# Attention in 32 items of a head pair and a query tile, halves of the array in turn, four banks for index scores

## What is computed

```python
proj = x @ w_in          # q, k, v of all branches, index q and k, and the gates
# A: for each query the 128 keys with the best index score
rel   = relu(einsum('bqhd,bsd->bqhs', q_idx, k_idx))          # 8 index heads of 32
score = where(pos_k <= pos_q, einsum('bqhs,bqh->bqs', rel, w_idx) * idx_scale, -inf)
sel   = top_k(score, 128);  softmax over the selected keys, with a slope per head
# B: window of 128 keys, a sink in the softmax, two query heads for one key head
# C: all earlier keys (with 512 tokens each query sees every earlier block), slope, softmax
# D: stick breaking, no softmax
z = q @ k.T * scale
log_keep  = where(pos_k < pos_q, log_sigmoid(-z), 0)
a = where(strict, exp(log_sigmoid(z) + cumsum_from_the_right(log_keep) - log_keep), 0)
y_d = a @ v
merged = sum_n(sigmoid(g_n) * (y_n @ w_branch_n));  out = merged @ w_out
```

## Time and profile before

| what | us |
|---|---|
| median of three runs | 1786.89 |
| time of the profiled execution | 1791.51 |
| its span, first to last instruction | 1789.5 |
| TensorE busy in the span | 1733.0 |
| DVE busy | 1354.5 |
| ACT busy | 766.8 |
| GpSimd busy | 756.8 |
| mean granted TensorE clock | 0.981 |

### The profile page before, as it was taken

How to read it: one execution, slowest core, us unless ns; L and a number is a source line. 1 busy time by engine, 2 the same in 40 slices (tenths; PEclk the granted TensorE clock), 3 DMA queues, 4 the chain that set the end, 5 groups by cost and what they waited for, 6 DMA issues and landing times.

```text
span 1789.5 us, 23990 instructions
## 1 busy us (share of the span) xinstructions
PE 1733.0 (97%) x8789; PEld 1504.8 (84%) x8789; DVE 1354.5 (76%) x2574; ACT 766.8 (43%) x1337; POOL 756.8 (42%) x426
## 2 busy tenths in 40 slices
PE   7999999989999999999999999989899999999995
PEld 5667777768888999999999999989788888888884
DVE  2358994372236599789888988778889898889888
ACT  4334344442223443675477377533334333333331
POOL 5222223234446467514522632356455465344333
PEclk9889999999999999999999999999999999999997
DMA  5111112124242356787588668999999999999991
GB/s 194 48 48 54 53 59 65 65 63 150 82 130 71 104 172 211 231 300 274 177 287 288 218 227 303 333 406 400 407 407 392 388 397 373 386 393 393 380 334 71
DMA packets 126355, 417.60 MB, mean 233 GB/s; under 512 B 12960, under 2 KB 32416, under 8 KB 124704
## 3 DMA queue, kind: packets, MB, share of 16 engines
q1 hardware_dynamic: 70176, 232.81, 36.6%
q0 software_dynamic: 36864, 134.23, 20.1%
q10 hardware_dynamic: 19200, 49.03, 7.4%
HBM read 364.91 MB, written 50.86 MB: 232 GB/s over the span
## 4 chain that ended last, share of the span: by engine, by line
PE 88%; DMA 5%; DVE 5%; ACT 1%; issue 1%; ACTq 0%; SPq 0%; DVEq 0%
PE ps L1276 16%; PE ps L1277 16%; PE ps L1278 16%; PE ps L1469 9%; PE ps L1470 9%; PE ps L1472 9%; PE ps L1568 5%; DMA gelu_in<-gelu_d 2%; PE ps L1348 2%; DMA u_got<-u_rows,eid 2%; PE ps L1392 2%; DMA raw<-u_units 1%; PE ps L1361 1%; PE ps L1367 1%; PE ps L1327 1%; DVE u_got L1070 1%
## 5 line engine op out<-in xcount | busy, mean ns | idle before, releaser
L1276 PE MATMUL ps<-tok_hi,w_hi 128*128 128x384 f32 (+2 forms) x1552 | 555.6, 358 | 17.5 <-DVE tok_lo L812 9.3
L1277 PE MATMUL ps<-tok_lo,w_hi 128*128 128x384 f32 (+2 forms) x1552 | 546.8, 352 | 0.0
L1278 PE MATMUL ps<-tok_hi,w_lo 128*128 128x384 f32 (+2 forms) x1552 | 546.4, 352 | 0.0
L537 ACT ACTIVATE w_hi<-raw 128x1024 fp32r<-128x1024 f32 x334 | 353.1, 1058 | 355.9 <-PE ps L1472 184.0
L437 POOL TENSOR_TENSOR w_lo<-raw,w_hi 128x1024 fp32r<-128x1024 f32 x80 | 194.0, 2429 | 365.2 <-ACT w_hi L537 365.0
L1276 PEld LDWEIGHTS ps<-tok_hi,w_hi 128*128 128x128 f32 x1552 | 295.9, 191 | 38.7 <-issue 11.8
L1278 PEld LDWEIGHTS ps<-tok_hi,w_lo 128*128 128x128 f32 x1552 | 295.7, 191 | 19.8
L1277 PEld LDWEIGHTS ps<-tok_lo,w_hi 128*128 128x128 f32 x1552 | 296.1, 191 | 17.9
L1469 PE MATMUL ps<-w_hi,gh_hi 128*128 128x512 f32 x768 | 299.8, 390 | 5.5 <-DVE gh_lo L1200 5.3
L1064 DVE TENSOR_TENSOR w_lo<-raw,w_hi 128x1024 fp32r<-128x1024 f32 x196 | 239.0, 1219 | 87.3 <-ACT w_hi L537 87.0
L493 POOL DMA_INDIRECT u_got<-u_rows,eid x128 | 169.1, 1321 | 309.1 <-DVE h_own L1070 298.6
(11 more groups left out here) (194 smaller groups left out, 1939.6 us busy)
## 6 DMA issues: line engine op xcount, KB each, us to landing
raw<-u_units SPq DMA_DIRECT2D x128, 512.0 KB, 4.1
raw<-v_rows SPq DMA_DIRECT2D x128, 512.0 KB, 8.5
raw<-w_units SPq DMA_DIRECT2D x78, 512.0 KB, 3.4
gate_d<-stage ACTq DMA_DIRECT2D x12, 2048.0 KB, 7.8
gelu_d<-gelu_t ACTq DMA_DIRECT2D x120, 192.0 KB, 4.0
gelu_in<-gelu_d SPq DMA_DIRECT2D x30, 768.0 KB, 9.3
gate_in<-gate_d SPq DMA_DIRECT2D x28, 768.0 KB, 15.5
gate_in<-gate_d SPq DMA_DIRECT2D x2, 1536.0 KB, 23.0
```

Of the source, the lines that this page charges most:

```text
L537: act.activation(w_hi[:, n % RAW, :], raw[:, n % RAW, :], ACT.Copy).then_inc(hi_done, 1)
L1276: pe.matmul(out_, l_hi, r_hi, start=start, stop=False)
L1277: pe.matmul(out_, l_hi, r_lo, start=False, stop=False)
L1278: return pe.matmul(out_, l_lo, r_hi, start=False, stop=stop)
```

## The change

The 16 heads become 8 pairs with 4 query tiles each, 32 items s, one per unit. For item s TensorE does scores of s+1, weights of s, outputs of s-1, the unit. Scores, probabilities, logarithms and `colw` of an item hold both heads side by side ([128, 2, 512]), and `row`, `ls` and `colw` are double. Where two operations of one engine were needed for two tiles of a head, one now takes both heads, except where a scale or a sum is per head. Head pair matmuls alternate between row halves (scores, banks 2 and 3) and column halves (outputs). D's scores now go by query tile, so a tile i has i+1 matmuls a head of 128 columns in place of one, and its sums (i+1)(i+2)/2 a head. B's heads are reordered to (0, 2, 1, 3), so that the two of a pair read different halves of the keys; the host permutes w_branch to match. Index scores take banks 2 to 5, and each waits for the relu four before it. V is transposed into the unit's own bank (n mod 2), and unit n+2 then waits for ACT to have read it. DVE's bias is computed for both heads, for A in each item.

```diff
-        [("B", h) for h in range(NH)] + [("A", h) for h in range(NH)]
+        [("B", h) for h in (0, 2, 1, 3)] + [("A", h) for h in range(NH)]
-    row = [at(f"row{i}", R + 84 + 5 * i, [P, 1280]) for i in range(4)]
-    colw = at("colw", R + 104, [P, 1280])
+    row = [at(f"row{i}", R + 84 + 4 * i, [P, 2, S]) for i in range(2)]
+    ls = [at(f"ls{i}", R + 92 + 4 * i, [P, 2, S]) for i in range(2)]
+    bias = ls[0]
+    colw = [at(f"colw{i}", R + 100 + 4 * i, [P, 2, S]) for i in range(2)]
...
@@ ACT @@
+            def exponents(s):
...
+                    act.wait_ge(nbias_set, soft_item(s) + 1)
+                    for ab in range(2):
+                        act.activation(row[s % 2][:, ab, :n], row[s % 2][:, ab, :n], ACT.Exp, scale=SCALE,
+                                       bias=nbias[:, ab, i:i + 1], accum_out=rsum[:, ab, i:i + 1]).then_inc(exp_done, 1)
...
+            def weights(s):
...
+                    act.wait_ge(t_full, s + 1)
+                    if s >= 2:
+                        act.wait_ge(pv_done, 2 * (s - 1))
+                    act.activation(colw[s % 2][:, :, :n], ps[:, 4:6, :n], ACT.Copy).then_inc(t_read_act, 1)
...
@@ DVE @@
+            def scores(s):
...
+                    dve.wait_ge(item_scores, 2 * (s + 1))
+                    dve.tensor_scalar(tmp[:, :, :n], ps[:, 2:4, :n], SCALE, None, ALU.mult).then_inc(item_read, 1)
...
+                    dve.scalar_tensor_tensor(ls[s % 2][:, :, :n], tmp[:, :, :n], -1.0, tmp[:, :, :n],
+                                             ALU.mult, ALU.min).then_inc(abs_set, 1)
...
+            for s in range(-1, N_ITEM):
+                if s + 1 < N_ITEM:
+                    scores(s + 1)
+                if s >= 0:
+                    weights(s)
+                if s >= 5 and s % 4 == 1:
+                    store_y(s // 4 - 1)
+                if s >= 0:
+                    for _ in range(2 + s % 2):
+                        if r < 3 * TOPK // 8:
+                            choose_keys(r)
+                            r += 1
+                if s + 1 < N_ITEM:
+                    scores_end(s + 1)
...
@@ TensorE @@
             def att_unit(n):
...
+                if n - 2 in V_UNITS:
+                    pe.wait_ge(vt_read, V_ORDER.index(n - 2) + 1)
...
             def index_scores(first):
...
-                    score_free(s)
-                    pe.matmul(score_bank(s)[:, :(t + 1) * P], projT[rows, 6 + h // 4, t * P:(t + 1) * P],
+                    if s >= 4:
+                        pe.wait_ge(relu_done, s - 3)
+                    pe.matmul(index_bank(s)[:, :(t + 1) * P], projT[rows, 6 + h // 4, t * P:(t + 1) * P],
...
+            def scores(s):
...
+                if s == 0:
+                    pe.wait_ge(relu_done, 3 * IH)
+                else:
+                    pe.wait_ge(item_read, s)
+                k0, n = keys_of(kind, i)
+                for kt in range(i + 1 if kind == "D" else 1):
+                    for ab in range(2):
+                        rows = slice(HD * ab, HD * ab + HD)
+                        q, k = projT[rows, q_slot, :], projT[rows, k_slot, :]
+                        if kind == "D":
+                            ins = pe.matmul(ps[:, 2 + ab, kt * P:(kt + 1) * P], k[:, kt * P:(kt + 1) * P], q[:, tile_],
+                                            start=True, stop=True)
+                        else:
+                            ins = pe.matmul(ps[:, 2 + ab, :n], q[:, tile_], k[:, k0:k0 + n], start=True, stop=True)
...
+            def weights(s):
...
+                if s >= 1:
+                    wait_t_read(s - 1)
+                if kind == "D":
+                    pe.wait_ge(softplus_set, s - 8 + 1)
+                    for ab in range(2):
+                        for kt in range(i + 1):
+                            for k2 in range(kt, i + 1):
+                                last = pe.matmul(ps[:, 4 + ab, kt * P:(kt + 1) * P],
+                                                 (neg_after if k2 == kt else neg_ones)[:],
+                                                 row[s % 2][:, ab, k2 * P:(k2 + 1) * P], start=k2 == kt, stop=k2 == i)
+                else:
+                    pe.wait_ge(probs_set, 2 * (soft_item(s) + 1))
+                    for ab in range(2):
+                        for j in range(keys_of(kind, i)[1] // P):
+                            block_ = slice(j * P, (j + 1) * P)
+                            last = pe.transpose(ps[:, 4 + ab, block_], row[s % 2][:, ab, block_], ident[:])
+                last.then_inc(t_full, 1)
+
+            def outputs(s):
...
+                for j in range(n // P):
+                    for ab in range(2):
+                        c0 = 0 if kind == "A" else HD * ab
+                        ins = pe.matmul(ps[HD * ab:HD * ab + HD, 6 + p % 2, i * P:(i + 1) * P],
+                                        v_tok[:, chunk, k0 // P + j, c0:c0 + HD], colw[s % 2][:, ab, j * P:(j + 1) * P],
+                                        start=j == 0, stop=j == n // P - 1)
...
+            for s in range(-1, N_ITEM):
+                n = N_FIRST + s
+                if s + 1 < N_ITEM:
+                    scores(s + 1)
+                if s >= 0:
+                    weights(s)
+                    if s >= 1:
+                        outputs(s - 1)
+                    if n < N_ATT:
+                        att_unit(n)
+                    if n - 1 in V_UNITS and n - 1 >= N_FIRST:
+                        v_to_tokens(n - 1)
+                for b in {29: (2, 3), 31: (1,)}.get(s, ()):
+                    branch(0, b)
+            outputs(N_ITEM - 1)
```

More of the change, by code:

```diff
@@ L846, in choose_keys @@
                     link(dve.tensor_tensor(left_over, left_over, dist[:, S - n:S], ALU.add))
[L848 to L851 removed]
+            def scores(s):
+                kind, i, p = kind_of(s), s % 4, s // 4
+                n = keys_of(kind, i)[1]
                 if kind != "D":
[L853 to L868 removed]
@@ new lines, in scores @@
+                    width = {"A": n, "B": 2 * P, "C": S}[kind]
+                    if s >= 2:
+                        dve.wait_ge(t_full, s - 1)
+                    dve.wait_ge(item_scores, 2 * (s + 1))
+                    for ab in range(2):
+                        ins = dve.tensor_tensor_reduce(
+                            out=row[s % 2][:, ab, :n], in0=ps[:, 2 + ab, :n], in1=bias[:, ab, width - n:width], scale=1.0,
+                            scalar=-3.0e38, op0=ALU.add, op1=ALU.max, accum_out=mx[:, ab, i:i + 1])
@@ L896, in scores_end @@
-                    link(dve.reciprocal(rinv[:, u % 2, two], rsum[:, u % 2, two]))
-                    for t in (2 * half, 2 * half + 1):
-                        n, o = keys_of(kind, t)[1], row_at(kind, t)
-                        dve.tensor_scalar(row[u % 2][:, o:o + n], row[u % 2][:, o:o + n], rinv[:, u % 2, t:t + 1],
+                        dve.wait_ge(sink_exp, 2 * (s - 16 + 1))
+                        link(dve.tensor_tensor(rsum[:, :, i], rsum[:, :, i], esink[:, :, i], ALU.add))
+                    link(dve.reciprocal(rinv[:, :, i], rsum[:, :, i]))
@@ L918, in weights @@
-            def weights(u, half):
-                if HEADS[u][0] != "D":
-                    return
-                for i in (2 * half, 2 * half + 1):
-                    kt = keys_scored(u, i)
-                    o, n = col_at(kt), S - kt * P
-                    idx = plan["u", u, i][0]
-                    dve.wait_ge(tp_full, idx + 1)
-                    dve.tensor_tensor(colw[:, o:o + n], ps[:, 4 + idx % 2, :n], row[2 + u % 2][:, o:o + n],
-                                      ALU.add).then_inc(tp_read_dve, 1)
+                    last = slice(i * P, (i + 1) * P)
@@ new lines, in scores_end @@
+                    softplus, logs = row[s % 2], ls[s % 2]
+                    dve.wait_ge(t_full, s - 1)
+                    dve.wait_ge(stick_ln, s - 8 + 1)
+                    link(dve.scalar_tensor_tensor(softplus[:, :, :n], tmp[:, :, :n], 0.0, logs[:, :, :n],
+                                                  ALU.max, ALU.add))
+                    dve.tensor_tensor(softplus[:, :, last], softplus[:, :, last],
+                                      seen[:].unsqueeze(1).to_broadcast([P, 2, P]), ALU.mult).then_inc(softplus_set, 1)
@@ L1630 @@
         [qb[:, :P], qb[:, P:], w["kb"], w["vb"]] + two("qa") + [cat(w["ka"], w["ka"])]
+    by_pair = a["w_branch"][0].copy()
+    by_pair[1] = by_pair[1].reshape(2, 2, HD, DM).transpose(1, 0, 2, 3).reshape(2 * P, DM)
     proj, units = iter(proj), []
```

370 lines of the change are left out of this document (116 added, 254 removed).

## The result

| | before | after |
|---|---|---|
| median of the runs, one comparison | 1786.57 us (1785.91 to 1789.42, 4 runs) | 1764.38 us (1761.96 to 1765.24, 4 runs) |
| profiled execution | 1791.51 | 1765.24 |
| its span | 1789.5 | 1763.2 |
| mean granted TensorE clock | 0.981 | 0.984 |

The ratio is 0.9863, with a 95% interval from 0.9846 to 0.9881: the kernel became faster by 1.4%, 24.5 us (21.3 to 27.5); the two medians differ by 22.2. The forecast was 1755, a gain of 31.8; the range of 1746 to 1774 holds the result. The two profiled executions differ by 26.3 us.

The account below looks back on a forecast made before the run. TensorE, busy 97% of the span, was taken as the bound. Gains of 18 (index scores and opening) and 17 (steps with a unit), less 4 (tail), gave 31 to 32 us off the 1786.9 median: 1755 us, range 1746 to 1774.

Parts of the forecast that it names:

- (a): Index scores, 33.9 to 85.2 us: four banks shorten six sets from 16.5 to 5.0 us, plus 3.5 from the clock.
- (b): Opening, 85.2 to 97.4 us: 12.1 us becomes about 9.3, gain 2.8, bounds 0 and 5.
- The slow units: Units at low clock after four index sets cost 7.0 us; bounds 0 and 7, half (3.5) taken as gain.
- (c): Steps with a unit, 97.4 to 354 us: paired scores and outputs overlap on array halves, net gain 17 us.
- I charge 4 us for both pairs, bounds 0 and 8: D's steps: TensorE waits for DVE's softplus in steps with tiles 1 and 2, costing 4 us.
- The stalls beside GpSimd: D's steps: one DVE pass stands still while GpSimd splits a weight, some 1.6 us a step, 6.4 per pair.
- (d): Tail, 354 to 371.7 us: item 31's chain lies open without units, cost 4 us, bounds 1 and 8.
- From 372 on nothing is touched, and it shifts: Everything after the attention, from 372 us on, keeps its length and only moves earlier.
- Rival 1: Outputs: column halves run one after the other, costing 15.8 us more; gain 20, 1767 us; chance 0.23.
- Rival 2: Neither 64-row halves nor column halves overlap; another 9 us lost, gain 11, 1776 us; chance 0.06.
- Rival 3: Each short matmul has a fixed cost of 12 ns, adding 2.1 us in the attention: 1757 us; chance 0.05.
- Rival 4: Clock falls in the items' steps, units cost 7.25 us in place of 5.5: 51 us, 1806 us; chance 0.06.

Follow-up runs that it names:

- the second and third execution of before: The kernel before, unchanged, profiled two more times in one execution each: 1789.87 and 1788.6 us.
- the moved choosing: Kernel after with DVE's 48 rounds of choosing placed elsewhere, none in the last nine items: 1760.99 us, ratio 0.9841 to the kernel before.

## Why the prediction was right and where not

**Bound, (a) and (b), predicted 18, measured 21.1.** The sets take 0.86, 0.64, 0.86, 0.86, 1.07 and 1.07 us, 5.4 in all where 5.0 was forecast (11.2 won); only the first takes 0.2 more than its columns and a start. The opening, from the last set's end to unit 9, takes 7.8 where 9.3 was forecast and 11.8 stood before: the wait for the relus is 2.07 as foreseen, and the softmax chain of two heads with 128 columns is shorter. Unit 9 stays slow (0.74), as forecast. The slow units were to give back half of 7.0 us. In this pair of executions they give back all that they cost, 6.4. (The 7.0 set 7.25, read from starts, against 5.5, read from the chain of waits; by starts a unit at full clock takes 5.66 to 5.69.) Against the other two executions of before unit 9 comes 18 us earlier, exactly the sum.

**The base.** "... which lies 4.6 us above the median of 1786.9. I subtract from the median", with half of the slow units given back, holds for the kernel as it mostly runs: the second and third execution of before have two slow units of 4 to 8, and the half was right on average, though for no reason that the prediction had. The median itself was low: three later comparisons gave 1788.46, 1789.46 and 1787.85. Some 2 of the 9.4 us between 1755 and 1764.4 are this. The other 7.3 are gain that wasn't there (31.8 against 24.5). Those two executions of before and the two of after differ by 23 to 25 us, the first pair by 26.3; the terms below give both where they differ.

**(c), predicted 17, measured 12.9** in the first pair of executions (256.8 to 243.9, from the first matmul of unit 9 to the end of unit 37) and 12.2 in the others. Here most of the miss lies. The halves are right to a few hundredths: scores of 512 columns 1.06 us, outputs of tile 3 1.02, where 1.1 and 1.0 stood. Taken away they cost 11.8 and 13.5 us, where 15.8 less DVE's waits was reckoned. In the chain of waits a unit behind the outputs takes 5.66 to 5.69 us, where one behind transposes took 5.49 (116.57 to 122.06 before); that is the 0.2 for the return to the full width, charged rightly. Four items of C take 31.2 us, the two heads took 34.4: the 3.2 of the sum. The step that failed is "I charge 4 us for both pairs, bounds 0 and 8": TensorE waited 5.6 there, and D's eight steps took 82.7 against 79.6 by the sum (four heads of 20.5, less twice 3.2, plus 4). The mechanism was the one foreseen, DVE late in the steps before the longer sums; the moved choosing removes it and wins 3.4 us. The stalls beside GpSimd, 1.6 a step or 12.8 by the sum, were 7 us in four of the eight steps; two of them fell on the mask that TensorE waits for. In the whole stage TensorE is idle for 6.1 us. Without that it would have won 19.1 where 21 were reckoned: the share of the first and last items that falls outside the stage, put at 2, was too small. Of three short waits for probabilities (1.4 us together, 5.6 less the tail's 4.2) only one, 0.5, lies in this stage; the others are in the opening and in the tail.

**(d), predicted 4, measured 4.8** (22.6 less 17.9). The forecast length was 21.9. The wait of 4.2 is near the working, but the clock wasn't in it: after the pause most of the pieces run at the lower clock, item 31's transposes 1.87 us instead of 1.02, item 30's outputs 1.48 instead of 0.81, and the stretch has 0.85 on average.

**"From 372 on nothing is touched, and it shifts"** is the other step that failed: 29.3 won at the merge, 26.3 at the end, and in the other executions 25.4 won at the start of the out product and 23.9 at the end. From there to TensorE's last instruction four executions with the old attention take 1267.9 to 1269.1 us, nine with the changed one 1269.0 to 1272.6 (the one with the scores on the same rows 1268.0). About 2 us are mostly lost there. The stretch from 1221 has a clock of 0.93 in the kernel after; at the same work the kernel before has 0.97, with the DMA queues as full:

```profile
1250.00:1300.00 50.00, 44.68 (x188) 35.85 (x188) 42.14 (x67) 16.33 (x21) 23.07 (x18) 0.97 1.03 407
```

But the clock isn't what is lost. Counted by the same matmul, the kernel after is ahead by 28.1 us at 1179.3, by 23.8 at 1246.9, and by 29.1 again at 1263.6. It is down to 26.5 at 1337.4, and from 1263.5 on both kernels have a clock of 1.00; only 1.1 us of it is a wait of TensorE, for DVE's `gh_lo`. What there depends on a start that is 25 us earlier stays open.

**The rivals.** Rival 1 (column halves in turn) is refuted by 1.02 against 1.89 us. The Trainium skill's page "TensorEngine Tiling (Array Packing)", Key Properties, was right about columns as about rows. Rival 2 falls with it. Rival 3: the 40 instructions of a tile's sums in D take 4.63 to 4.72 us and start 0.112 us apart, those of outputs on one half 0.109 to 0.110, where 128 columns need 0.107. So each has a cost of its own of 2 to 5 ns, not 12. The 60 cycles that the Trainium skill's page "TensorEngine Tiling (Array Packing)", Instruction Overhead, gives don't show in any row. Rival 4 (the clock falls in the items): 0.99 from 75.9 to 319.8, and 1.00 in D, with four changes of width a step.

The sign, the range and the order of the parts came out right. The likeliest value was 9.4 us too low: some 2 us by the base, 4 to 5 in the steps with a unit (3 of them D's), 1 in the tail, and 1.5 to 3 beyond the attention. That (a) and (b) fit is luck in part: half of the slow units was right without a reason, and the opening won 1.2 us more than its term.

## What to carry to other kernels

Matmuls that use half of the array's rows or columns are worth pairing, and they should be issued in turn, at least every four instructions; check the result by the distance of starts of the whole run, against the same run on one half. Before a large rewrite try its smallest part alone: more banks, so that TensorE doesn't stop for a reader, were nearly half of the gain here. Where a stretch of low clock is part of the sum, look at it in more than one execution before it is priced.

## What was not expected of the hardware

- A half of the array runs ahead of the program's order by about four instructions of 128 columns and not further: 4 a head cost nothing in the wrong order, 6 cost 0.27 (columns) and 0.32 us (rows), 8 cost 0.49 and 0.55.
- The lower clock comes in the same code in one execution and not in the next: four, two and two of units 4 to 8 in three executions of before, and one (unit 8, 8.43 us) with two banks in the kernel after, at the same pauses.
- A pass of DVE that stood still beside GpSimd's subtraction ended 0.0 to 0.8 us after it in the attention of the kernel after, far beyond its own length: 0.42 us became 2.47 here as 0.29 became 2.05. Not every pass does so: 16 of 31 subtractions stretched none.
